# Experts of a mixture-of-experts layer in fp32 on four column groups, packed by load

## The reference

```python
def moe_swiglu(h, router, wg, wu, wd):
    logits = (h @ router).astype(jnp.float32)
    top_v, top_i = lax.top_k(logits, TOP_K)
    top_w = jax.nn.softmax(top_v, axis=-1)
    comb = jnp.sum(jax.nn.one_hot(top_i, N_EXPERTS, dtype=jnp.float32) * top_w[..., None], axis=-2)
    out = jnp.zeros(h.shape, jnp.float32)
    for e in range(N_EXPERTS):
        out = out + comb[..., e:e + 1] * swiglu(h, wg[e], wu[e], wd[e]).astype(jnp.float32)
    return out.astype(h.dtype)
```

## Time and profile before

| | before |
|---|---|
| median of 3 runs | 1832.25 us (1831.83 to 1832.76) |
| span of the profiled execution | 1830.0 us |
| TensorE busy, its matmuls | 1808.3 us, 99% |
| TensorE's weight loads (beside its matmuls) | 1466.8 us, 80% |
| VectorE busy | 1445.7 us, 79% |
| ScalarE busy | 1134.4 us, 62% |
| GpSimd busy | 175.0 us, 10% |
| moved by DMA | 494.72 MB, mean 270 GB/s |

### The profile page before, as it was taken

How to read it: one execution, slowest core, us unless ns; L and a number is a source line. 1 busy time by engine, 2 the same in 40 slices (tenths; PEclk the granted TensorE clock), 3 DMA queues, 4 the chain that set the end, 5 groups by cost and what they waited for, 6 DMA issues and landing times.

```text
span 1830.0 us, 26449 instructions
## 1 busy us (share of the span) xinstructions
PE 1808.3 (99%) x10038; PEld 1466.8 (80%) x10038; DVE 1445.7 (79%) x1414; ACT 1134.4 (62%) x1092; POOL 175.0 (10%) x171
## 2 busy tenths in 40 slices
PE   8999999999999999999999999999999999999998
PEld 7878777788888787677888888888888888888886
DVE  5688576654556786666998988989989899898898
ACT  5575334443444763244777777777777777777775
POOL 1362004000001630031000000000000000000100
PEclk9999999999999999999999999999999999999999
DMA  9642224554566332236999999999999999999994
GB/s 348 198 167 93 93 93 174 204 184 156 189 211 215 134 138 94 93 108 251 364 373 377 390 344 386 368 373 388 357 377 376 376 387 364 356 377 365 394 412 167
DMA packets 193048, 494.72 MB, mean 270 GB/s; under 512 B 7913, under 2 KB 14693, under 8 KB 176937
## 3 DMA queue, kind: packets, MB, share of 16 engines
q1 hardware_dynamic: 187616, 479.61, 71.5%
q0 software_dynamic: 2640, 9.77, 1.4%
q10 hardware_dynamic: 2680, 3.74, 0.6%
HBM read 482.03 MB, written 7.34 MB: 267 GB/s over the span
## 4 chain that ended last, share of the span: by engine, by line
PE 91%; DVE 5%; ACT 2%; issue 1%; DMA 0%; SPq 0%; DVEq 0%
PE bank L1962 50%; PE bank L1367 28%; PE bank L1582 2%; PE bank L1359 2%; PE bank L1553 1%; PE bank L1976 1%; PE bank L1928 1%; DVE ring_lo L2034 0%; DVE tmp L2034 0%; DMA ring<-w_in_dram 0%; DVE xterm L2034 0%; DVE xc L2398 0%; DVE y_rwkv L2034 0%; PE bank L1505 0%; PE bank L1528 0%
## 5 line engine op out<-in xcount | busy, mean ns | idle before, releaser
L2034 DVE TENSOR_TENSOR w_lo<-ring,w_hi 128x2048 fp32r<-128x2048 f32 x288 | 656.0, 2290 | 75.9 <-ACT w_hi L1256 62.8
L1256 ACT ACTIVATE w_hi<-ring 128x2048 fp32r<-128x2048 f32 x264 | 506.3, 1918 | 100.6 <-PE bank L1962 96.0
L1962 PE MATMUL bank<-w_hi,xg_hi 128*128 128x512 f32 x896 | 352.8, 394 | 1.2 <-DVE xg_lo L2648 1.2
L1962 PE MATMUL bank<-w_lo,xg_hi 128*128 128x512 f32 x896 | 349.0, 389 | 0.9 <-issue 0.9
L1962 PE MATMUL bank<-w_hi,xg_lo 128*128 128x512 f32 x896 | 349.3, 390 | 0.0
L1962 PEld LDWEIGHTS bank<-w_hi,xg_hi 128*128 128x128 f32 x896 | 168.3, 188 | 35.5 <-DVE xg_lo L2648 1.4
L1962 PEld LDWEIGHTS bank<-w_hi,xg_lo 128*128 128x128 f32 x896 | 168.2, 188 | 35.6
L1962 PEld LDWEIGHTS bank<-w_lo,xg_hi 128*128 128x128 f32 x896 | 168.4, 188 | 35.2 <-issue 1.3
L1962 PE MATMUL bank<-w_hi,ehT_hi 128*128 128x512 f32 x448 | 176.2, 393 | 0.0
L1962 PE MATMUL bank<-w_hi,ehT_lo 128*128 128x512 f32 x448 | 174.6, 390 | 0.0
L1962 PE MATMUL bank<-w_lo,ehT_hi 128*128 128x512 f32 x448 | 174.5, 389 | 0.0
(11 more groups left out here) (464 smaller groups left out, 3067.3 us busy)
## 6 DMA issues: line engine op xcount, KB each, us to landing
ring<-moe_w_gate_dram SPq DMA_DIRECT2D x96, 1024.0 KB, 7.1
ring<-moe_w_up_dram SPq DMA_DIRECT2D x96, 1024.0 KB, 7.4
ring<-moe_w_down_dram SPq DMA_DIRECT2D x96, 1024.0 KB, 7.1
ring<-w_in_dram SPq DMA_DIRECT2D x25, 2048.0 KB, 9.1
spare<-moe_w_up_dram SPq DMA_DIRECT2D x16, 1024.0 KB
spare<-moe_w_gate_dram SPq DMA_DIRECT2D x16, 1024.0 KB
spare<-moe_w_down_dram SPq DMA_DIRECT2D x16, 1024.0 KB
ring<-w_branch_dram SPq DMA_DIRECT2D x6, 2048.0 KB, 7.5
```

What stands on the lines that cost most here:

```text
L1256: A.activation(w_hi[:, q % PARTS, :], slot_half(q), ACT.Copy).then_inc(s.hi_ready, 1)
L1962: ins = M(dst, a, w, start=start and n == 0, stop=stop and n == 2, skip_group_check=True)
L2034: return V.tensor_tensor(out_, a, b, op)
```

## The change

Only the second layer's experts and what leads to them are changed.

- Items are pairs of 96 and 64 places. VectorE sorts the experts by load; the four with most tokens take the first places of the pairs, the others the second. What does not fit goes to further items of up to 96 and 64 tokens.
- The products are plain fp32, with no splitting of weights or activations. 32 tokens are the stationary operand, and four matmuls go to the four 32-column groups of the array, each with 256 other columns of the weights (128 in the last round); their outputs lie in partitions 0 to 31, 32 to 63 and so on. A 96-token item does this three times for each chunk, a 64-token item twice.
- The host lays each expert's weights out as 42 halves of 1 MB, in the order of use, a partition's 8 KB together (`expert_halves`). The gate and up columns go in four rounds of 1024, 1024, 1024 and 512.
- There are 14 slots of 1 MB. SyncE issues a half when TensorE has finished with the one 14 before it (`half_done`). The first 14 wait for the tiles of the mixers whose place they take (`first_free`).
- ScalarE and VectorE only copy or multiply out of PSUM. The transposes are 21 and 14 to an item, of 128 x 128. Outputs are stored by four DMAs an item.
- The rows of zeros come from an input by one DMA of SyncE during the first layer; before, GpSimd cleared and stored them at the router.
- The last item's output is scattered by 16 matmuls of 32 rows, the row groups of the array side by side.
- The routing arithmetic on VectorE is longer: a sort and the items before and behind `select`, places and weights after the first gather.

The diff, its core:

```diff
...
+CAP = (96, 64)
+GROUPS = (3, 2)
+GROUP = 32
+SEL = CAP[0] + CAP[1]
...
-EP = 21
-HALVES = 14 + 13
-SURE = NE
-SLOTS = 7
+FURTHER = 6
+ITEMS = NE + FURTHER
+HALVES = 42
+SLOTS = 14
+ROUNDS = 4
+ZERO_ROW = SEL * ITEMS // 2
+EY_ROWS = ZERO_ROW + 32
+ALWAYS_STORED = SEL * (PAIRS - 1) + CAP[0]
...
-    w_hi = sb("w_hi", [P, PARTS, HALF], F32R, where=X)
-    w_lo = sb("w_lo", [P, PARTS, HALF], F32R, where=X + 24576)
...
+    ring_half = [[ring_at + SLOT * 4 * ((NPAN - 3 + i) % RING) + HALF * 4 * r for r in range(2)] for i in range(3)]
+    slot_at = [B + 45056, pr_at, B + 24576, B + 32768, scratch, *ring_half[0], E, E + 8192, ec_at, *ring_half[1],
+               *ring_half[2]]
+    slots = [sb(f"slot{i}", [P, HALF], where=w) for i, w in enumerate(slot_at)]
...
+            if n == PANELS.index(("gate", 0, 3, 1)):
+                sp.dma_start(ey_rows[ALWAYS_STORED:EY_ROWS, :], zeros[:, :]).then_inc(s.ey_stored, 16)
...
+        def half(e, q):
+
+            sp.dma_start(slots[q % SLOTS][:], moe_halves[e, q:q + 1].rearrange("o q (p n) -> p (o q n)", p=P))\
+                .then_inc(half_loaded[q % SLOTS], 16)
+
+        def first_free(q):
+
+            if q == 0:
+                sp.wait_ge(s.product_ready, JOB_AT["Y11.1"] + 1)
+            elif q == 1:
+                sp.wait_ge(s.rwkv_done, 2 * T)
+            elif q == 2:
+                sp.wait_ge(s.product_ready, JOB_AT["br111.1"] + 1)
+            elif q == 7:
+                sp.wait_ge(s.merged_done, 2 * 2 * T)
+            elif q in (10, 12):
+                sp.wait_ge(*used_up(NPAN - 2 + (q - 10) // 2))
+
+        for q in range(HALVES):
+            if q == SLOTS:
+                sp.wait_ge(s.ey_stored, 16)
+            if q < SLOTS:
+                first_free(q)
+            else:
+                sp.wait_ge(s.half_done, q - SLOTS + 1)
+            half(slice(0, 1), q)
...
+        def item_halves(e, pair, k):
+
+            for q in range(HALVES):
+                sp.wait_ge(s.half_done, pair * (2 * HALVES) + (HALVES * k + q - SLOTS + 1))
+                half(bass.ds(e, 1), q)
+                if q == 15:
+                    rows_, groups = CAP[1 - k], GROUPS[1 - k]
+                    sp.wait_ge(s.ey_ready, pair * 2 + (k + 1))
+                    for p in range(4):
+                        dst = ey_rows[bass.ds(pair * SEL + (0 if k == 1 else CAP[0] - SEL), rows_), 256 * p:256 * p + 256]
+                        sp.dma_start(dst.rearrange("(g k) n -> k g n", k=GROUP),
+                                     ey[GROUP * p:GROUP * p + GROUP, 0:256 * groups]
+                                     .rearrange("k (g n) -> k g n", n=256)).then_inc(s.ey_stored, 16)
...
-        def three(dst, x_hi, x_lo, b, k, start, stop):
-
-            pairs = ((x_hi, w_hi[:, b, k]), (x_hi, w_lo[:, b, k]), (x_lo, w_hi[:, b, k]))
-            for n, (a, w) in enumerate(pairs):
-                ins = M(dst, a, w, start=start and n == 0, stop=stop and n == 2, skip_group_check=True)
-            return ins
...
+        def gathered_tokens(x, pair):
+
+            if x < 3:
+                pe.wait_ge(s.act_xg_ready, pair * 3 + (x + 1))
+            elif x in (3, 6):
+                pe.wait_ge(s.vec_xg_ready, pair * 2 + x // 3)
...
-                            for c in range(4):
-                                x = 4 * r + c
-                                if k == q // 2 == x % 2 == 0:
-                                    pair_read_out(pe, pair, f"gx{x // 2}", 1)
-                                ins = three(b[:], xg_hi[:, k, x, :], xg_lo[:, k, x, :], q % PARTS,
...
+                            w = slots[q % SLOTS][:].rearrange("p (c q n) -> p c q n", c=chunks_, q=4)
+                            for c in range(chunks_):
+                                x = chunks_ * m + c
+                                if k == r == g == 0:
+                                    gathered_tokens(x, pair)
+                                for i in range(GROUPS[k]):
+                                    o = CAP[0] * k + GROUP * i
+                                    to = base + width * i
+                                    for p in range(4):
+                                        ins = M(psum[GROUP * p:GROUP * p + GROUP, to:to + width], xg[:, x, o:o + GROUP],
+                                                w[:, c, p, :], start=x == 0 and to % 512 == 0, stop=x == KD - 1,
+                                                skip_group_check=True)
+                            ins.then_inc(s.half_done, 1)
...
+                for j in range(14):
+                    q = 28 + j
+                    if j == 3:
+                        turn(pair, k, 3)
+                    half(q)
+                    w = slots[q % SLOTS][:].rearrange("p (c q n) -> p c q n", c=2, q=4)
+                    for c in range(2):
+                        x = 2 * j + c
+                        if x % 8 == 0:
+                            pe.wait_ge(s.eht_ready, pair * 8 + (4 * k + x // 8 + 2))
+                        for i in range(GROUPS[k]):
+                            o = 1536 * k + 256 * (k + 1) * i
+                            for p in range(4):
+                                ins = M(psum[GROUP * p:GROUP * p + GROUP, o:o + 256], ehT[:, x, GROUP * i:GROUP * i + GROUP],
+                                        w[:, c, p, :], start=x == 0 and o % 512 == 0, stop=x == 27, skip_group_check=True)
+                    ins.then_inc(s.half_done, 1)
+                    if j == 4 and k and not last:
+                        pe.wait_ge(s.sel_ready, pair + 2)
+                        gather(0)
...
+        step(stt(out=e8(1), in0=b[:, 16:24], scalar=8.0, in1=C("order"), op0=ALU.mult, op1=ALU.subtract))
...
+        free(V.tensor_copy(e8(0), b[:, 16:24]), "rank.1")
+        settle()
+        step(tt(pick[:, 0], square(e8(1)), wide(e8(1), NE), ALU.is_gt))
+        settle()
+        step(V.reduce_sum(e8(2), pick[:, 0], AX.X))
+        settle()
+        step(tt(onehot[:], square(e8(2)), wide(C("rank"), NE), ALU.is_equal))
+        settle()
+        step(tt(pick[:], by_tile(onehot[:]), by_item(R(5), NE), ALU.mult))
+        settle()
+        step(V.reduce_sum(spos[:, :, 0:NE], pick[:], AX.X))
...
-                for q in range(PARTS, 2 * EP):
-                    lo(q)
...
+def expert_halves(gate, up, down):
+
+    def of(w, c0, cols, chunks_):
+        w = w[:, :, c0:c0 + cols].reshape(NE, KD // chunks_, chunks_, P, cols)
+        return w.transpose(0, 1, 3, 2, 4).reshape(NE, KD // chunks_, P * HALF)
+
+    parts = []
+    for r in range(ROUNDS):
+        for w in (gate, up):
+            parts.append(of(w, 1024 * r, 1024 if r < 3 else 512, 2 if r < 3 else 4))
+    parts.append(down.reshape(NE, 14, 2, P, D).transpose(0, 1, 3, 2, 4).reshape(NE, 14, P * HALF))
+    return np.ascontiguousarray(np.concatenate(parts, 1))
...
```

More of the change, by code:

```diff
@@ L35 @@
 HALF = SLOT // 2
-PARTS = 3
 QUARTER = SLOT // 4
@@ L513, in build @@
[L513 to L520, removed]
-    spos = sb("spos", [P, 3, T, NE], where=X + 116096)
-    comb = sb("comb", [P, 3, T, NE], where=X + 116352)
@@ L523, in build @@
[L523 to L530 removed]
+    NPAN = len(PANELS)
@@ L531, in build @@
+    place_f = tab("place_f", [P, 2, 2 * T])
+    weight = tab("weight", [P, T])
+    items = tab("items", [1, 16], I32)
+    pairs_of = tab("pairs_of", [1, 4], I32)
+    assert small[0] <= ec_at and ec_at == scratch + 14592 + 4096, (small[0], ec_at)
+    ey_rows = nc.dram_tensor("ey_rows", [EY_ROWS, D], F32, kind="Internal").ap()
+    back = [sb(f"back{j}", [P, T, D], where=w) for j, w in enumerate((hn_at, E + 65536))]
+    fin = sb("fin", [P, T, D], where=ehT_at)
     assert B + 53248 + 4096 <= int(nc.sbuf_usable_end), (B, int(nc.sbuf_usable_end))
@@ new lines, in turn_of_two @@
+                glus(pe, pair, 4 * k + 3)
+                for j in range(14):
[17 more added lines that the diff above has]
+                        gather(0)
+                    if j == 4 and k and last:
+                        pe.wait_ge(s.last_sel_ready, 1)
+                        for g in range(2):
+                            for t in range(T):
+                                ins = TR(banks[7][:, SEQ * g + P * t:SEQ * g + P * t + P],
+                                         sel4[:, t, P * g:P * g + P], ident)
+                        ins.then_inc(s.sel_turned, 1)
@@ L2021, in _ @@
+            if not last:
+                pe.wait_ge(s.act_xg_ready, pair * 3 + 6)
+                pe.wait_ge(s.vec_xg_ready, pair * 2 + 4)
         with nc.Fori(0, last_pair, engines=bass.OrderedEngineSet([pe.engine]), hint_back_edge=True) as pair:
@@ L2606, in select @@
[L2606 removed]
+                    ins = ts(sel[:, t, CAP[0] * k:CAP[0] * k + CAP[k]], C("slots", 0, CAP[k]),
+                             column(spos, at_of(ITEMS * t + k)), None, ALU.is_equal)
             ins.then_inc(s.sel_ready, 1)
[L2609 to L2613 removed]
+        select(lambda i: slice(i, i + 1))
@@ L2737, in add_back, with last_item @@
```

(19 more changed lines are left out.)

736 lines of the change are left out of this document (325 added, 411 removed).

## The result

| | before | after |
|---|---|---|
| median of all runs | 1832.25 us (5 runs) | 1722.73 us (5 runs) |
| ratio, 95% interval | | 0.9389 [0.9374, 0.9405] |
| the same kernel again (e1_again) | 1831.14 us | 1717.96 us (4 runs), 0.9382 [0.9363, 0.9402] |
| span of the profiled execution | 1830.0 us | 1715.0 us |
| TensorE | 1808.3 us | 1640.6 us |

The kernel became 110 to 113 us faster; 132 were forecast. One of the five executions of the changed kernel ran at a granted clock of 0.75 from end to end and took 2084 us, so the ratio is of the other four, whose median is 1720.6 us, and the rows of after come from another execution of the same kernel, e1_again, at 0.99.

What follows compares the result with a forecast made beforehand. TensorE bounded the kernel before; weight transfers were to bound the experts after the first item. That item ends at 978 us, transfers and stores reach 1683, last half 1687, tail 10.7: span 1698, forecast 1700 us, range 1678 to 1765.

Steps and rivals of the forecast that it cites:

- Start and first item: Router to first expert item: first expert matmul at 865 us, the 96-token item 113 us, over at 978.
- The set: Expert matmuls on TensorE: four matmuls of 32 tokens on four column groups take 434 ns, bounds 430 and 860.
- rival (a): Expert matmuls: column groups do not all run at once; no faster at 545 ns a set, 2360 us at 860; chance 0.10.
- The rate: Expert weight transfers: 421 GB/s, 2.49 us a half of 1 MB, bounds 408 (2.57) and 432 (2.43).
- rival (b): Weight transfers at 408 GB/s instead of 421, giving 1722 us, or at 432, 1683; within the forecast's 0.67.
- the sum of the transfers: Experts after 978 us: 281 halves x 2.49 = 700 us, stores 5, to 1683; 1687 with latency and last matmuls.
- TensorE's margin: Each pair of expert items: TensorE needs 192 us, the transfers 211, so the transfers bound.
- Rival (d): TensorE's instructions come late: at 1 us a packet, a set of 496 ns and 1750 us; 0.14 shared with (c).
- Rival (c): Clock falls to 1.2 GHz while TensorE waits for DMA in 64-token items: 1720 to 1745 us; 0.14 shared with (d).
- A sign that misleads: Profile after, weight queue: it was to wait for TensorE only up to 980 us; waiting throughout would show (a).
- The tail: Last expert matmul to the kernel's end: 10.7 us taken, 10 to 12 expected.

Runs made afterwards that it cites:

- e1_again: The changed kernel once more, unaltered, run for a profile at the full granted clock: 1717.96 us, ratio 0.9382 to the kernel before.
- e3: The changed kernel with only the first 512 KB of each half loaded from the fifteenth on, TensorE's work unaltered: 1666.53 us, ratio 0.9099 to the kernel before.
- e9: The changed kernel with its seven output stores cut to 32 rows of four 16-byte pieces, zero fill enlarged: 1715.94 us, ratio 0.9358 to the kernel before.

## Why the prediction came out as it did

The forecast was 1700 with a range of 1678 to 1765, and its mechanism is what happened: fp32 sets at 434 ns, transfers as the bound behind the first item, VectorE and ScalarE without part in it. That the time came within 23 us is in part luck, since two errors of its largest term went opposite ways. Point by point:

- **Start and first item.** First expert matmul at 863 (865 forecast, 864.25 before); the item took 115 (113), so it was over at 978 as forecast. Right.
- **The set.** 434.6 ns (434). The choice of the nearest row for four streams was right and rival (a) has no part. The Trainium skill ("TensorE: Matmul & The Clock Gate", Part 3, packing small matmuls) gives 2.38 for three column tiles, which as a rate would have been 544 ns a set; e1_again measured 434.6 with four groups over runs of 48 sets, so read as a rate of long runs the Trainium skill's figure does not hold here.
- **The rate.** 2.49 us a half was forecast, 2.44 is the distance of undisturbed landings: 430 GB/s, next to the upper bound of rival (b), 432. The Trainium skill's some 358 GB/s of HBM for a core ("DMA: Bandwidth & Descriptors", Specifications) is well under the 424 of the profile's slices; the Trainium skill, in the section Bandwidth of the same page, gives it as a core's share when both cores that share an HBM stream, and this kernel runs on one core.
- **The step that was mis-sized** is the sum of the transfers: 281 halves at 2.49 us, 700, and 5 us of stores, to 1685 with the last half's latency. The last half landed at 1701.7, 16.6 us later. Two terms carry it. At 978 three or four halves were in flight and not one (the 57th landed at 989.1, where the sum has 983): 6 us, less the 2.2 that I had allowed for latency. And the 279 halves from there took 712.6 us, not 700. At 2.44 they alone are 681, 14 us less than at 2.49. The other 32 us, where the sum has 5, are in e1_again's landings 19 us of the twelve late ones at every eighth instruction packet, 6 us where the rows are fetched back (2.1 MB, 1625 to 1656 us, which the sum forgot), and 7 us of smaller delays whose cause wasn't traced. The stores are in these delays; e9 prices them at 4.4, and without them the twelve cost 15. So the rate was better than forecast by 14 us, and the traffic beside the weights dearer by 27: half of that miss was made good by luck.
- **TensorE's margin.** 192 us a pair were forecast, e3 measured 193 to 199, 198 on average, the gap at the back edge and the late instructions within. The transfers take 84 x 712.6 / 279 = 214.5 a pair, where 211 were forecast, so it costs nothing, and the margin is some 17 us in place of 19.
- **Rival (d)**, late instructions, was half right: they come late by all signs, 26.2 + 5.7 us in the unaltered kernel, but the transfers hide it; what they cost is on the other side, in the queue of the weights. It had been priced only as a wait of TensorE.
- **Rival (c)**, the clock, was seen and hidden. In the window with the stop at the back edge (columns as above) the granted clock is 0.74 where it is 1.00 before:

```profile
1040.00:1060.00 20.00, 19.30 (x319) 12.36 (x318) 1.15 (x2) 1.10 (x4) 0.00 (x0) 1.00 1.01 424
1060.00:1080.00 20.00, 14.34 (x186) 8.10 (x190) 0.00 (x0) 0.46 (x1) 0.00 (x0) 0.74 1.01 424
...
1065.00:1070.00 5.00, 4.35 (x34) 1.67 (x35) 0.00 (x0) 0.00 (x0) 0.00 (x0) 0.50 1.01 424
```

  The 5 us behind the stop are at 0.50, the lower level of 1.2 GHz, and from 1075 it is 1.00 again. GB/s stays at 424 through it. Waits of 0.5 us in each 2.45, which the rival feared, left the clock at 1.00 (1660 to 1700 us).
- **A sign that misleads.** I wrote that the queue would wait for TensorE only up to 980. It does all the way, 352 us in 188 waits (820 to 1715 us):

```profile
SPq L744 <- PE bank L1953: 242.0, 134, 4.8
SPq L744 <- PE bank L1973: 110.0, 54, 2.7
```

  At 1100, 1300 and 1500 us nine or ten halves are issued and not yet landed, so the DMA engines have work while the queue waits for a slot, and its wait says nothing of the bound. The GB/s line does.
- **The tail** was 13.3 us after the last landing, 12.4 forecast.

## What to carry to other kernels

Before fp32 on column groups takes the place of three passes, count the groups: here a set of four is 434 ns, so it wins at 20 groups of 32 tokens and loses by 257 us at 32. Where items of unlike weight alternate in front of a bound of transfers, the buffers must hold the difference between them, and a light item at the start gained nothing while a heavy one stood at the end; light ones at both ends weren't tried. And a kernel of many small matmuls pays for its instructions in the weights' own queue: price fetches, stores and gathers on the DMA side before calling a sum of transfers done.

## What was not expected of the hardware

- TensorE stops for 5.2 and 4.2 us at the loop's back edge, all operands there (TensorE's timeline of e1_again at the first):

```profile
1057.79 1.93 PE L1973 MATMUL bank<-slot,ehT 128*32 128x256 f32 x32 [0.42 <-DMA slot<-moe_halves_dram]
1064.88 4.47 PE L1953 MATMUL bank<-slot,xg 128*32 128x256 f32 x34 [5.16 <-issue]
```

  A 16 KB instruction packet starts at 1062.1 and takes 0.9 us. Shorter stops of 0.6 to 2.5 us come mostly at the end of the last SwiGLU round, where a matmul has 128 columns and instructions are used up twice as fast.
- Every eighth instruction packet goes with a half that lands 1.2 to 1.7 us late (31 intervals in three traces).
- Three matmuls in a row to one column group make a set 47% longer (637 against 434.6 ns), two change nothing (440 against 438).
- Rows of 8 KB move at 424 GB/s and rows of 2 KB at 405, under the same backlog.
